# Feed forward projections of a decoder layer: two weight chunks multiplied in turn, one matmul each

## The reference, cut to what matters

```
h = rmsnorm(x, ffn_norm)
u = causal_dwconv(h @ w_up, conv_ff) + conv_ff_bias      # w_up 1024 x 5632, width 3
ug, uv = split(u, 2)
x = x + (silu(ug) * uv) @ w_down                          # w_down 2816 x 1024
```

## Time and profile before

| | |
|---|---|
| median of 3 runs | 1159.39 us (1157.6 to 1159.72) |
| the profiled execution, its own time | 1160.82 us |
| its span, first to last instruction | 1159.0 us |
| TensorE busy | 1123.9 us, 97% of the span |
| VectorE, GpSimd, ScalarE busy | 655.2, 633.1 and 549.4 us |
| mean granted TensorE clock | 0.995 |

### The profile page before, as it was taken

How to read it: one execution, slowest core, us unless ns; L and a number is a source line. 1 busy time by engine, 2 the same in 40 slices (tenths; PEclk the granted TensorE clock), 3 DMA queues, 4 the chain that set the end, 5 groups by cost and what they waited for, 6 DMA issues and landing times.

```text
span 1159.0 us, 16765 instructions
## 1 busy us (share of the span) xinstructions
PE 1123.9 (97%) x5502; PEld 898.7 (78%) x5502; DVE 655.2 (57%) x1036; ACT 549.4 (47%) x886; POOL 633.1 (55%) x769
## 2 busy tenths in 40 slices
PE   6998989999999999999999999999999999999997
PEld 4786667777777777667878888888888888888886
DVE  4668976767666776862213324476776515731534
ACT  5584647566565656551322124544444314433542
POOL 6386264546554564645456554566576754573452
PEclk9999999999999999999999999999999999999999
DMA  8354031331404123213223523333333432332232
GB/s 243 77 132 130 26 94 35 85 85 35 102 18 118 38 64 100 75 54 85 79 77 105 181 72 91 91 93 114 103 90 91 116 102 73 109 96 80 74 89 79
DMA packets 196619, 104.36 MB, mean 90 GB/s; under 512 B 3926, under 2 KB 195401, under 8 KB 196553
## 3 DMA queue, kind: packets, MB, share of 16 engines
q1 hardware_dynamic: 196172, 103.39, 32.0%
q10 hardware_dynamic: 381, 0.15, 0.1%
HBM read 101.40 MB, written 2.13 MB: 89 GB/s over the span
## 4 chain that ended last, share of the span: by engine, by line
PE 87%; DVE 9%; ACT 3%; issue 1%; ACTq 0%; DVEq 0%
PE bank L562 75%; PE bank L698 2%; PE bank L712 1%; DVE prod L1810 1%; DVE xs L1812 1%; PE bank L705 1%; PE bank L657 1%; DVE pr L1722 1%; PE bank L922 1%; DVE pr L1721 0%; DVE oa_lo L1978 0%; PE bank L909 0%; PE bank L919 0%; PE bank L910 0%; PE bank L913 0%
## 5 line engine op out<-in xcount | busy, mean ns | idle before, releaser
L492 POOL TENSOR_TENSOR w_lo<-w_raw,w_hi 128x256 fp32r<-128x256 f32 x692 | 549.9, 828 | 259.9 <-ACT w_hi L1074 254.2
L562 PE MATMUL bank<-hn_hi,w_hi 128*128 128x512 f32 x1000 | 408.4, 408 | 1.0 <-DVE o_a L1985 1.0
L562 PE MATMUL bank<-hn_hi,w_lo 128*128 128x512 f32 x1000 | 391.0, 391 | 0.0
L562 PE MATMUL bank<-hn_lo,w_hi 128*128 128x512 f32 x1000 | 390.4, 390 | 0.0
L562 PEld LDWEIGHTS bank<-hn_hi,w_hi 128*128 128x128 f32 x1000 | 189.0, 189 | 43.7 <-issue 9.2
L562 PEld LDWEIGHTS bank<-hn_hi,w_lo 128*128 128x128 f32 x1000 | 187.9, 188 | 40.4
L562 PEld LDWEIGHTS bank<-hn_lo,w_hi 128*128 128x128 f32 x1000 | 188.7, 189 | 34.6 <-issue 1.7
L507 POOL CAST w_hi<-w_raw 128x1024 fp32r<-128x1024 f32 x70 | 78.2, 1117 | 222.0 <-PE bank L562 131.3
L1074 ACT ACTIVATE w_hi<-w_raw 128x1024 fp32r<-128x1024 f32 x111 | 117.9, 1062 | 77.6 <-PE bank L562 69.7
L2096 DVE SCALAR_TENSOR_TENSOR u<-vr,pt,u 128x511 f32<-128x511 f32 x88 | 88.9, 1010 | 8.3 <-DVE u L2096 0.7
L2090 DVE TENSOR_TENSOR vr<-bank,rs 128x512 f32<-128x512 f32 x44 | 30.4, 692 | 72.5 <-PE bank L562 67.1
(11 more groups left out here) (308 smaller groups left out, 1643.6 us busy)
## 6 DMA issues: line engine op xcount, KB each, us to landing
w_raw<-in_w_in SPq DMA_DIRECT2D x73, 512.0 KB, 6.7
w_raw<-in_w_up SPq DMA_DIRECT2D x44, 512.0 KB, 3.8
w_raw<-in_w_down SPq DMA_DIRECT2D x16, 512.0 KB, 3.9
crow<-cum_rows_out SPq DMA_DIRECT2D x16, 256.0 KB, 5.7
w_raw<-in_w_br_a SPq DMA_DIRECT2D x8, 512.0 KB, 4.0
w_raw<-in_w_br_b SPq DMA_DIRECT2D x8, 512.0 KB, 4.0
w_raw<-in_w_out SPq DMA_DIRECT2D x8, 512.0 KB, 3.9
w_raw<-in_w_ple_gate SPq DMA_DIRECT2D x8, 512.0 KB, 4.0
```

The lines of the kernel that those rows point to most:

```text
L492: ins = pool.tensor_tensor(wlo[c.slot][:, ks, :], raw[c.slot][:, ks, :], whi[c.slot][:, ks, :].bitcast(F32), ALU.subtract)
L562: mm = pe.matmul(acc, w[c.slot][:, i, :], xx[:, x0 + i, :], start=(i == 0 and n == 0), stop=last)
```

## The change

In the up and down projections PE takes two chunks at a time and issues their matmuls alternately, one of the first, one of the second. The first chunk's bank and the second's alternate with them. The order of the matmuls within a chunk stays. Of part 0 of the up projection the first two chunks are still taken one after the other.

```
-            def gemm(c, x_hi, x_lo, k=KD, x0=0, more=None, ready=None):
+            def gemm(c, x_hi, x_lo, k=KD, x0=0, more=None, ready=None, each=False):
...
-                    if i < k - 1:
+                        if each and not last:
+                            yield
+                    if i < k - 1 and not each:
                         yield
...
+            def run_two(one, other):
+
+                for _ in zip(one, other):
+                    pass
...
-                        for q in range(1, 4):
-                            run(gemm(stream.up[0].at(q), hn_hi, hn_lo))
+                        run(gemm(stream.up[0].at(1), hn_hi, hn_lo))
+                        run_two(*[gemm(stream.up[0].at(q), hn_hi, hn_lo, each=True) for q in (2, 3)])
                     with pe.Fori(1 if part == 0 else 0, k // 2) as n:
-                        for q in range(4):
-                            run(gemm(stream.up[part].at(q, n), hn_hi, hn_lo))
+                        for q in (0, 2):
+                            run_two(*[gemm(stream.up[part].at(q + r, n), hn_hi, hn_lo, each=True) for r in range(2)])
...
                     with pe.Fori(0, KD // 4) as n:
-                        for q in range(4):
-                            run(gemm(stream.down[part].at(q, n), fa_hi, fa_lo, k, first_k))
+                        for q in (0, 2):
+                            run_two(*[gemm(stream.down[part].at(q + r, n), fa_hi, fa_lo, k, first_k, each=True) for r in range(2)])
```

## The result

The changed kernel takes 1203.76 us (median of 4 runs, 1199.56 to 1204.43) where the kernel before takes 1159.2 (here of 4 runs): the ratio is 1.038, with a 95% interval of 1.0363 to 1.0398. That is 44.6 us more. The direction and the waits were as forecast, but the forecast was 1189.4 with a range up to 1202. The profiled execution took 1204.43 us, 43.6 more than that of before.

What follows compares the result with a forecast made beforehand. TensorE's matmuls were taken to bound the kernel, 97% busy. Eleven waits of 2.5 us (27.5) plus small terms of 2.5 gave +30 us on the median of 1159.39, so 1189.4 us, with a range from 1178 to 1202.

Steps and rivals of the forecast that it cites:

- What bounds, and what alternating gives: Feed forward: PE's matmuls set the end; alternating banks was taken to change their 0.2267 us spacing by 0.
- The row at the bank change: Earlier trace, 863.53 to 863.75: starts 0.22 us apart across a bank change, so the switch costs and gives nothing.
- When chunk 2p+5 is wanted and ready: Up pairs: pair p+2's second chunk has its weights due at E + 10.94 but ready at E + 13.02.
- E: The end of the last matmul of chunk b, the second chunk of pair p; times are counted from it.
- the contention: `gate_low` beside POOL's pieces for chunk 2p+5: POOL or DVE may lose 0.44 us, so 2.23 to 2.67 in two pairs.
- The term 11 x 2.5 = 27.5: Up parts: a PE wait at every other pair, 8 and 3 steps, 2.5 us each, 27.5 us (24.5 to 29.4).
- The small terms, 2.5: Start, end of part 0, down 2, tail and two entries of down loops: together 2.5 us more.
- The clock falls as well: Rival: some 2 us at half clock follow each of 11 waits, about 1 us each; 1195 to 1208 us, chance 0.13.
- Faster matmuls: Rival: alternating banks brings matmuls toward the 0.2133 us bound; 1179 to 1184 us, chance 0.06.
- a shorter path: Rival: faster taps or hidden `gate_low` make chunk 2p+5 ready by E + 11.7 to 12.6; 1171 to 1181 us, chance 0.08.
- no loss: Rival: nothing waits in the up pairs, so the time stays 1159.4 us; chance of not slower 0.05.
- "not slower" case: Rival: chunk 2p+5 ready by E + 10.94, needing 2.1 us less path in all 22 pairs; 1159.4 us, chance 0.05.

Runs made afterwards that it cites:

- the filled kernels: Changed kernel plus five or two matmuls, written to an unread bank, in each alternated up pair: 1192.9 us with five, 1192.16 us with two.
- The earlier ACT order: Changed kernel with each high part of the up and down parts made one place earlier in ACT's list: 1161.72 us, ratio 1.002.
- `gate_low` moved: Changed kernel with `gate_low` moved on DVE from between the next pair's two scalings to behind its own pair's last product: 1180.91 us, ratio 1.0188.
- threes: Changed kernel, but PE switches between the two chunks after three matmuls instead of after each: 1181.84 us, ratio 1.0208.
- two added matmuls: Changed kernel plus two matmuls, written to an unread bank, in each alternated up pair: 1192.16 us, ratio 1.0288.

## Why the prediction was wrong

*What bounds, and what alternating gives.* Right. The row at the bank change held for 1008 matmuls: no price and no gain. With the banks alternating too, a pair's matmuls follow each other at 0.227 us. The Trainium skill's 215.7 ns (TensorE: Matmul & The Clock Gate, "Back-to-back issue gap") is not what they do; the section calls it the gap of an isolated matmul and has some 131 ns for a stream of weight loads and matmuls of 512 columns, with which the trace doesn't agree either.

*When chunk 2p+5 is wanted and ready.* Right as a path. Up to the high part it came out to 0.05 us (E + 10.17 against 10.12), in part by luck: the four taps took 4.19 us and not 4.58, and the first product, beside a piece of POOL's, 1.11 and not 0.69. PE's start is at E + 13.69 against 13.07 without contention. Of the 0.62 us over, 0.49 lie in POOL's four pieces, one of them beside `gate_low`, and 0.08 between their end and PE's start (0.13 against 0.05). I had bounded the contention at 0.44 and taken 0.27 of it. DVE's instruction kept its 0.69 here, and POOL paid. The rule of the Trainium skill (SBUF — State Buffer, "Who interferes with whom"), that a VectorE instruction with two SBUF inputs contends with a GpSimd one that reads SBUF, agrees with the trace in kind: the piece beside `gate_low` took 1.26 us, the one before it, beside the scaling of a with its product from a bank, 0.73.

*The price of the waits.* The term 11 x 2.5 = 27.5 measured 30.8, so it was mis-sized by 3.3 us. The number of waits, 8 and 3, and their place at every other pair are as worked out. The small terms, 2.5, measured about 2.

*The clock.* This is the step that failed. "The clock falls as well" stood as a rival with a chance of 0.13 and 1195 to 1208 us, and the forecast took 1.00. The rival is what happened, together with the forecast's own waits: seven falls of 1.61 us, 11.3 us. I had priced the rival at 11 falls of 1 us; that this makes about the same sum is luck, since each fall costs more and there were fewer. The trace of before had one case of a fall behind a wait of 2.09 us, and I discounted it on the ground that here dense matmuls stand around the wait. No row carried that. Without the clock the forecast would have been 3 us off, as the filled kernels show (1192.2 and 1192.9). The range then cut off the rival's upper half, where the result lies.

*Rivals.* Faster matmuls, a shorter path and no loss did not happen. The earlier ACT order shows what the "not slower" case needed: chunk 2p+5 in time in all pairs. It needs no faster engine, only another order of ACT's list.

## What to carry to other kernels

If two accumulations are interleaved, the second one's operands are needed a whole accumulation earlier and the first one's result comes a whole accumulation later; work out for each producer whether its place in its engine's program still meets this, and move it together with the change. Here one line's place on ACT was worth 42 us. When the sum contains waits of TensorE like these, about 2 us and coming back regularly, price the clock as part of the forecast and not as an accident, above all if the trace of before has one case of it.

## What was not expected of the hardware

- The clock's fall behind a wait is not decided by the wait's length alone. Of waits of 2.59 or 2.60 us in the changed kernel some are followed by it (872.23) and some are not (898.48, 923.12), and one of 1.91 us is (1005.68). In the feed forward of the profiled executions with `gate_low` moved, with threes and with two added matmuls, none fell; most of their waits are of 1.4 to 1.7 us, the longest 1.76, 1.96 and 2.12. What decides between these cases stays open.
- The number of falls seems to change from one execution to the next. The profiled execution of the changed kernel has a mean granted clock of 0.985 and took 1204.43 us; another has 0.989 and took 1199.56. With threes the slowest, 1185.66 us, has 0.991, where the profiled one has 0.995 and 1180.31. Only one execution of each kernel has a trace, so this is not shown.
- Adding 23.8 us of matmuls to a kernel in which TensorE is busy 95% of the time made it 10.9 us faster, since they kept the clock up in a stretch whose pace another engine set.
- An overlap of POOL's subtraction with DVE's work may be paid by one or by both: the piece beside `gate_low` took 1.26 us instead of 0.73 while `gate_low` kept its 0.69, and the first product at 812.99 took 1.11 instead of 0.69 beside a piece of POOL's in a row of four that took 4.37 us, where four alone take 2.82. The earlier trace rows has a like subtraction of DVE at 1.11.
